# Handing x and the norm weights over with columns on partitions, in a hybrid HGRN2 / latent-attention block on one core

## The reference

```
h   = rms_norm(x, attn_norm_w)
hq, hf, hi, hg, c_q, c_kv, k_r = split(h @ w_in)                 # 4 x 1024, 512, 512, 64
o_a = hgrn2(hq, hf, hi, hg)          # gated linear recurrence, 8 heads of 128, chunks of 64
o_b = latent_attention(rms_norm(c_q, ..) @ w_uq, rms_norm(c_kv, ..) @ w_ukv, k_r)   # 8 heads
x   = x + concat([o_a, o_b]) @ w_out
h   = rms_norm(x, ffn_norm_w)
x   = x + (silu(gate) * up) @ w_down        # gate, up = split(h @ w_gate_up), 5632 each
```

## Time and profile before

| | us |
|---|---|
| median of 3 runs | 1115.05 |
| lowest, highest | 1113.57, 1115.18 |
| the profiled execution | 1115.01 |
| its span from first to last instruction | 1113.3 |
| PE busy | 1103.5 |
| DVE busy | 900.2 |
| ACT busy | 644.7 |
| POOL busy | 61.0 |
| DMA, mean rate over the span | 207 GB/s |

### The profile page before, as it was taken

How to read it: one execution, slowest core, us unless ns; L and a number is a source line. 1 busy time by engine, 2 the same in 40 slices (tenths; PEclk the granted TensorE clock), 3 DMA queues, 4 the chain that set the end, 5 groups by cost and what they waited for, 6 DMA issues and landing times.

```text
span 1113.3 us, 15363 instructions
## 1 busy us (share of the span) xinstructions
PE 1103.5 (99%) x5176; PEld 927.6 (83%) x5176; DVE 900.2 (81%) x1234; ACT 644.7 (58%) x910; POOL 61.0 (5%) x154
## 2 busy tenths in 40 slices
PE   8999999999999999999999999999999999999998
PEld 7988888888888888888888888888888878888887
DVE  6688787587876577588988888988988889999887
ACT  7566777668654466365455555554554555655553
POOL 4200000000000000000000000000000020000000
PEclk9999999999999999999999999999999999999999
DMA  8766455554655455767777777787777786666665
GB/s 269 209 187 200 146 169 157 157 162 152 230 183 172 164 176 171 227 218 224 234 236 225 228 233 220 230 240 218 233 237 228 233 290 210 200 215 202 197 205 170
DMA packets 107557, 230.01 MB, mean 207 GB/s; under 512 B 8265, under 2 KB 19314, under 8 KB 107250
## 3 DMA queue, kind: packets, MB, share of 16 engines
q1 hardware_dynamic: 101346, 209.30, 60.3%
q0 software_dynamic: 5856, 19.93, 5.7%
q10 hardware_dynamic: 304, 0.14, 0.0%
HBM read 218.85 MB, written 10.49 MB: 206 GB/s over the span
## 4 chain that ended last, share of the span: by engine, by line
PE 91%; DVE 4%; DMA 2%; ACT 1%; issue 1%; SPq 0%; DVEq 0%; ACTq 0%
PE side L1975 22%; PE main L1731 20%; PE side L1977 11%; PE main L1734 10%; PE side L1945 4%; PE side L1946 4%; PE side L1947 4%; PE main L1945 3%; PE main L1946 3%; PE main L1947 3%; DMA raw<-in_w_down 1%; PE main L1751 1%; PE side L1773 1%; DVE w_lo L1122 1%; PE side L1870 1%
## 5 line engine op out<-in xcount | busy, mean ns | idle before, releaser
L1013 ACT CAST w_hi<-raw 128x1024 fp32r<-128x1024 f32 x245 | 239.8, 984 | 162.8 <-PE side L1975 62.8
L1573 DVE TENSOR_TENSOR w_lo<-raw,w_hi 128x1024 fp32r<-128x1024 f32 x245 | 274.6, 1133 | 17.7 <-ACT w_hi L1013 17.5
L1122 DVE TENSOR_TENSOR w_lo<-raw,w_hi 128x1024 fp32r<-128x1024 f32 (+3 forms) x156 | 178.8, 1156 | 97.1 <-ACT w_hi L793 94.4
L793 ACT CAST w_hi<-raw 128x1024 fp32r<-128x1024 f32 (+3 forms) x156 | 153.4, 993 | 130.2 <-PE main L1731 125.4
L1731 PE MATMUL main<-w_hi,hT_hi 128*128 128x512 f32 (+2 forms) x416 | 161.2, 388 | 0.2 <-issue 0.2
L1734 PE MATMUL main<-w_hi,hT_lo 128*128 128x512 f32 (+2 forms) x416 | 157.6, 380 | 0.0
L1975 PE MATMUL side<-w_hi,hT_hi 128*128 128x512 f32 x400 | 155.6, 389 | 0.0
L1977 PE MATMUL side<-w_hi,hT_lo 128*128 128x512 f32 x400 | 155.6, 389 | 0.0
L1731 PE MATMUL main<-w_lo,hT_hi 128*128 128x512 f32 (+2 forms) x416 | 107.1, 379 | 0.0
L1975 PE MATMUL side<-w_lo,hT_hi 128*128 128x512 f32 x400 | 106.9, 389 | 0.0
L1731 PEld LDWEIGHTS main<-w_hi,hT_hi 128*128 128x128 f32 x416 | 78.2, 188 | 13.2 <-issue 0.4
(11 more groups left out here) (292 smaller groups left out, 1887.5 us busy)
## 6 DMA issues: line engine op xcount, KB each, us to landing
raw<-in_w_gate_up SPq DMA_DIRECT2D x176, 512.0 KB, 4.8
raw<-in_w_down SPq DMA_DIRECT2D x88, 512.0 KB, 4.5
raw<-in_w_in SPq DMA_DIRECT2D x64, 512.0 KB, 4.0
raw<-in_w_out SPq DMA_DIRECT2D x32, 512.0 KB, 3.6
raw<-in_w_in SPq DMA_DIRECT2D x15, 384.0 KB, 5.0
squares<-hiddenT POOLq DMA_DIRECT2D x11, 512.0 KB, 5.3
hiddenT<-squares POOLq DMA_DIRECT2D x44, 128.0 KB, 5.2
raw<-in_w_ukv SPq DMA_DIRECT2D x8, 512.0 KB, 4.0
```

The source lines that it names most:

```text
L793: copy(w_hi[:, slot, 0:n], raw[:, slot, 0:n]).then_inc(s_hi, 1)
L1013: copy(w_hi[:, n % RING, 0:cols], src).then_inc(s_hi, 1)
L1122: tt(w_lo[:, slot, 0:n], raw[:, slot, 0:n], w_hi[:, slot, 0:n].bitcast(F32), ALU.subtract)\
L1573: tt(w_lo[:, n % RING, 0:cols], src, w_hi[:, n % RING, 0:cols].bitcast(F32), ALU.subtract)\
```

## The change

The host hands over a further array, `columns` (128 x 4137): for each partition 41 norm weights (attn, ffn, q latent, kv latent, hgrn) and then x with its columns on partitions, 16 tiles of 256 tokens. It is loaded in nine pieces into the place of `hT_lo`; the norm weights land in `vec_cols` with the first piece. ACT makes `hT_hi` from it and DVE makes `hT_lo` in place, so step `x` has no part for PE, and both steps `vec` are gone. The weights of g0 are issued by ACT, beside the first piece by SP. The load of g2 stands one place further ahead in SP's order.

`X` in rows is still needed for the squares and for the residual. It is loaded in four chunks of 512 columns behind g11, g12, g14 and g16; `sq1` moves to positions 10, 12, 13 and 15, `r1a` and `r1b` to 16 and 17. Since `lat_in` of block 0 (position 11) is now ahead of `r_in`, it copies; the squares of `lat_a` are scaled by `r_in`, and `lat_b` multiplies by both factors. The small loads that are left (positions, q_head and k_head weights) go behind g18, g19 and g20.

`sums_in` waits for a count of its own before each of the ten token sums (`SUMS_FROM`), where it waited once for each chunk (0, 2, 4, 6, 8 granules into the down projection).

```
+SUMS_FROM = (0, 0, 4, 8, 13, 19, 25, 31, 37, 43)
...
-X_AFTER = {1: (2,), 2: (3,), 3: (4,), 4: (5,), 5: (6,), 6: (7,), 7: (8,)}
-
-X_TURNED = (FIRST, -1, 1, 2, 3, 4, 5, 6, 7)
+XT_AFTER = {1: (1,), 2: (2,), 3: (3, 4), 4: (5,), 5: (6,), 6: (7,), 7: (8,)}
+X_AFTER = {11: 0, 12: 1, 14: 2, 16: 3}
+SMALL_AFTER = 18
...
-    s = [(FIRST, ("vec", 0))] + [(at, ("x", p)) for p, at in enumerate(X_TURNED)]
-    s += [(2 * c + 3, ("sq1", c)) for c in range(4)]
-    s += [(10, ("r1a",)), (11, ("r1b",)), (19, ("vec", 1))]
+    s = [(at, ("sq1", c)) for c, at in enumerate((10, 12, 13, 15))]
+    s += [(16, ("r1a",)), (17, ("r1b",))]
...
+        def load_tokens(p):
 
             k, wide = PIECES[p]
-            cols = slice(P * k, P * (k + wide))
-            engine.dma_start(X[:, :, cols], x_v[:, :, cols]).then_inc(s_x[p], 16)
+            c0, c1 = V_ROWS + SEQ * k if p else 0, V_ROWS + SEQ * (k + wide)
+            nc.sync.dma_start(x_columns[:, c0:c1], columns[:, c0:c1]).then_inc(s_xt[p], 16)
...
-            load_x(sp, 0)
-            for g, (b, k, n) in enumerate(GRANULES):
-                kind, i, w, c0, cols, rows, _ = BLOCKS[b]
+            load_tokens(0)
+            for g in range(1, G0):
...
+                for p in XT_AFTER.get(g, ()):
+                    load_tokens(p)
+
+                if g in X_AFTER:
+                    cols = slice(NB * X_AFTER[g], NB * (X_AFTER[g] + 1))
+                    sp.dma_start(X[:, :, cols], x_v[:, :, cols]).then_inc(s_x[X_AFTER[g]], 16)
...
-            pool.wait_ge(s_x[len(PIECES) - 1], 16)
+            pool.wait_ge(s_x[3], 16)
...
-                pool.wait_ge(s_used, W1 + 2 * c)
                 for n, p in enumerate(CHUNKS[c]):
+                    pool.wait_ge(s_used, W1 + SUMS_FROM[p])
...
-                elif kind == "x":
-                    ps, (k, wide) = filled(s), PIECES[a[0]]
-                    split_hi([(hT_hi[:, k + n, :], ps[:, n * SEQ:(n + 1) * SEQ], V_ATTN + k + n) for n in range(wide)])
+                if kind == "x":
+                    k, wide = PIECES[a[0]]
+                    act.wait_ge(s_xt[a[0]], 16)
+                    split_hi([(hT_hi[:, k + n, :], x_turned(k + n), V_ATTN + k + n) for n in range(wide)])
...
-                        square(latents[i][:, t, :], sumsq[:, t:t + 1])
+                        square(latents[i][:, t, :], sumsq[:, t:t + 1], scale=r_in[:, t:t + 1])
...
-            act.dma_start(vec_rows[0:KT, :], attn_norm_w.rearrange("a (k p) -> (a k) p", p=P)).then_inc(s_attn, 16)
-            load_x(act, 1)
+            load_granule(act, 0)
...
+                    for n in range(k, k + wide):
+                        ins = stt(out=hT_lo[:, n, :], in0=x_turned(n), scalar=vec_cols[:, V_ATTN + n:V_ATTN + n + 1],
+                                  in1=hT_hi[:, n, :].bitcast(F32), op0=ALU.mult, op1=ALU.subtract)
...
-                        ts(v, v, inv[:, t:t + 1], None, ALU.mult).then_inc(s_lat, 1)
+                        ts(v, v, inv[:, t:t + 1], r_in[:, t:t + 1], ALU.mult, ALU.mult).then_inc(s_lat, 1)
```

More of the change, by code:

```diff
@@ L274, in schedule @@
     s += [(e + 3, ("r2a",)), (e + 4, ("r2b",))]
+    s += [(at, ("x", p)) for p, at in enumerate(X_SPLIT)]
     return sorted(s, key=lambda x: x[0])
@@ L290, in steps_at @@
     return [step for p, step in SCHEDULE if p == position]
-def split_steps_at(position):
-    own = [step for step in steps_at(position) if step[0] != "x"]
-    return own + [("x", p) for p, at in enumerate(X_SPLIT) if at == position]
 def side_uses(step):
     kind = step[0]
-    if kind in ("x", "x2", "lat_t", "o_t"):
+    if kind in ("x2", "lat_t", "o_t"):
         return [(step, "dve")]
-    if kind in ("vec", "turn", "probs_t", "join7", "join8"):
+    if kind in ("turn", "probs_t", "join7", "join8"):
         return [(step, "act")]
@@ L359, in split_needed, with hybrid_layer @@
     return SPLIT[("x", len(PIECES) - 1)] + 1
-def hybrid_layer(nc, x, positions, attn_norm_w, w_in, hgrn_lb, hgrn_norm_w, mla_q_norm_w, w_uq, mla_kv_norm_w,
-                 w_ukv, q_head_norm_w, k_head_norm_w, w_out, ffn_norm_w, w_gate_up, w_down, out):
+def hybrid_layer(nc, x, columns, positions, w_in, hgrn_lb, w_uq, w_ukv, q_head_norm_w, k_head_norm_w, w_out, w_gate_up,
+                 w_down, out):
     weights = {"w_in": w_in[0], "w_uq": w_uq[0], "w_ukv": w_ukv[0], "w_out": w_out[0]}
@@ L381, in hybrid_layer @@
         hT_hi = sb("hT_hi", [P, KT, SEQ], F32R)
+        loaded = ctx.enter_context(ExitStack())
+        x_columns = sb("x_columns", [P, GAP + KT * SEQ], F32, loaded)[:, GAP - V_ROWS:]
+        loaded.close()
+        sb("vec_cols", [P, GAP])
+        vec_cols = x_columns[:, 0:V_ROWS]
         hT_lo = sb("hT_lo", [P, KT, SEQ], F32R)
@@ L494, in hybrid_layer @@
         s_tlo = sem("s_tlo")
-        s_x = [sem(f"s_x{p}") for p in range(len(PIECES))]
-        s_attn = sem("s_attn")
+        s_xt = [sem(f"s_xt{p}") for p in range(len(PIECES))]
+        s_x = [sem(f"s_x{c}") for c in range(4)]
         s_small = sem("s_small")
@@ L1050, in _ @@
                     convert(n % RING, loads(n), n, granule_size(n))
-                for s in split_steps_at(g):
+                for s in steps_at(g):
                     step(s)
@@ L1777, in step @@
                 kind, a = s[0], s[1:]
[L1778 to L1792 removed]
+                if kind == "x2":
                     c, j = a
@@ L1914, in lhs_of @@
                 return (mT_hi, mT_lo, ks) if kind == "uq" else (hT_hi, hT_lo, ks)
-            for g in range(FIRST, 0):
-                for s in steps_at(g):
-                    step(s)
             for g, (b, k, n) in enumerate(GRANULES):
@@ L2068, in granule_size @@
     return n * BLOCKS[b][4]
-_INS = ["x", "positions", "attn_norm_w", "w_in", "hgrn_lb", "hgrn_norm_w", "mla_q_norm_w", "w_uq", "mla_kv_norm_w",
-        "w_ukv", "q_head_norm_w", "k_head_norm_w", "w_out", "ffn_norm_w", "w_gate_up", "w_down"]
+_INS = ["x", "columns", "positions", "w_in", "hgrn_lb", "w_uq", "w_ukv", "q_head_norm_w", "k_head_norm_w", "w_out",
+        "w_gate_up", "w_down"]
 def kernel(**inputs):
@@ L2081 @@
     rows = np.concatenate([np.arange(P), np.arange(SEQ - 1, P - 1, -1)])
+    laid = {**inputs, "x": inputs["x"][:, rows], "positions": inputs["positions"][:, rows]}
+    norms = [inputs[f"{n}_w"][0].reshape(-1, P).T
+             for n in ("attn_norm", "ffn_norm", "mla_q_norm", "mla_kv_norm", "hgrn_norm")]
+    x_columns = laid["x"][0].T.reshape(KT, P, SEQ).transpose(1, 0, 2).reshape(P, KT * SEQ)
+    laid["columns"] = np.concatenate(norms + [x_columns], axis=1)
     for name in _INS:
-        a = np.ascontiguousarray(inputs[name][:, rows] if name in ("x", "positions") else inputs[name])
+        a = np.ascontiguousarray(laid[name])
         arrays[f"in_{name}"] = a
```

70 lines of the change are left out of this document (26 added, 44 removed).

## The result

| | us |
|---|---|
| kernel before, median (lowest to highest) | 1114.37 (1113.41 to 1115.18) |
| changed kernel, median (lowest to highest) | 1120.82 (1119.56 to 1121.52) |
| ratio, 95% interval | 1.0055 [1.0043, 1.0067] |
| profiled execution before, and its span | 1115.01, 1113.3 |
| profiled execution after, and its span | 1121.52, 1119.8 |

A forecast was written before the change was run, and what follows sets the result against it. TensorE, busy 1103.5 of 1113.3 us, was taken as the bound. Gains of 3.0 (start), 0.26 (norm-weight transpose) and 1.3 (token sums), 4.56 us in all, from 1115.0 gave 1110.5 us, range 1109.0 to 1112.8.

The forecast's parts named there:

- Term 1: Start, first lat block: without the transposes of x, lat 1 begins at 24.5 for 27.53, a gain of 3.0 us.
- the 7.95 that the bytes gave: Start: 236 KB less ahead of w_in for g2, 0.65 us at 373 GB/s, so it lands at 7.95, not 8.60.
- The rule of the Trainium skill that spoke against it: Loads of x: rows off 256 B boundaries need an extra transaction, an estimated 0.4 us; left out of the sum.
- The first matmul of all: Sign at the start: TensorE's first matmul was to come before 4.6 us.
- rival (a): Start: TensorE stays longer at its lower clock, g2 at 0.32 us a matmul, 1112.0 to 1112.3 us; chance 0.17.
- the seven granules' 2.08 us each: First lat block from g2 on: seven undisturbed granules on TensorE at 2.08 us each, 14.56 us.
- Term 2: After the pass at 47.09: the second transpose of norm weights goes, a gain of 0.26 us in full.
- Part 3: Lat blocks: x rows loaded later, squares later, r_in applied later, GpSimd starting at about 33 us; cost 0.
- rival (c): First lat block: holes keep TensorE at its lower clock, 1.8 us more per granule, 1117.6 with four; chance 0.04.
- Term 3: Head of the down projection: token sums loaded singly no longer delay w_down; gain 1.3 us, between 0.3 and 1.8.
- Rival (d): Lat blocks: x rows come late and ScalarE stands at the squares, two us at most, 1112.5 us; chance 0.06.

The follow-up runs named there:

- the start alone: Changed kernel with hT_lo 256 bytes on, GpSimd released by the last x piece in columns, token sums' loads at their old wait: 1111.22 us, ratio 0.9974.
- the kernel with the load early: Changed kernel with hT_lo 256 bytes on and GpSimd's 512 KB load of hgrn_lb released by the last x piece in columns: 1112.5 us, ratio 0.9985.
- the place mended: Changed kernel with hT_lo 256 bytes further on than before the change, not 192 (gap of 64 floats): 1113.06 us, ratio 0.9989.
- the kernel with both edits: Changed kernel with hT_lo 256 bytes on and GpSimd released by the last x piece in columns: 1110.18 us, ratio 0.9958.
- POOL early alone: Changed kernel with GpSimd waiting for the last piece of x in columns, not the last chunk in rows: 1118.01 us, ratio 1.0032.

## Why the prediction was wrong

**Term 1, the start: right, and a little too small.** Forecast 3.0 us with g9 at 24.5; it came at 24.14, and alone it is worth 3.2 us. w_in for g2 was on chip at 6.99 us (the start of its cast), not at the 7.95 that the bytes gave:

```profile
6.99 0.83 ACT L802 CAST w_hi<-raw 128x768 fp32r<-128x768 f32 x1 [1.15 <-DMA raw<-in_w_in]
8.11 0.91 ACT L849 ACTIVATE hT_hi<-x_columns 128x256 fp32r<-128x256 f32 x2 [0.30 <-DMA x_columns<-in_columns]
```

The piece of x behind it then became the last thing to arrive, so of these 1.6 us only 1.2 reached PE (9.16 for 10.34). The rule of the Trainium skill that spoke against it (page "DMA: Bandwidth & Descriptors", section "How a descriptor splits into AXI transactions") left no mark on this start: by it the term would have been 2.6 us, and from 12 to 15 us, with the new rows of x among the loads, the DMAs moved 384 GB/s for the 373 of the earlier trace rows. The first matmul of all came at 4.93, not before 4.6; it mattered nothing, as the working said. Matmuls in g2 took 0.21 us, then 0.18, and not 0.32: rival (a) did not occur in this execution. It did in others. With the start alone the first pass of g2 went at 0.31 us a matmul, and in the kernel with the load early all of g2 went at 0.32 us or more, so that lat 1 began 2.35 us later than here:

```profile
11.20 1.49 PE L1763 MATMUL main<-w_hi,hT_lo 128*128 128x384 f32 x4
...
26.49 0.33 PE L1743 MATMUL main<-w_hi,hT_hi 128*128 128x384 f32 x1
```

So the start's gain varies from run to run. Of the seven granules' 2.08 us each became 2.11; that was the place of `hT_lo` (with the place mended it is 2.08 again), visible here and not in my sum.

**Term 2, 0.26 us: right.** From the start of that pass to the next product it is 44.65 - 44.07 = 0.58 us now, where it was 47.94 - 47.09 = 0.85. It is inside the 3.2 us of the start alone.

**Part 3 failed, at its last sentence**: "so it is done by 33 + 17 = 50; DVE waits for its constants first at 72.87: 0." The time was right (51.55). What was wrong was to ask only who waits for POOL's results. POOL's work has a price for whoever works beside it. Its clears held DVE for 2 us at the one spot where PE comes to DVE's result with no slack left, and its 512 KB load moved among w_in's. The runs price it at 2.8 us (1120.82 to 1118.01), most of it the clears (2.2). The working also missed that this slack itself had shrunk. Before, `lat` was ready at 50.79 + 0.88 = 51.67 for a PE that came at 53.33. With the start 3 us sooner PE comes near 50.1, but DVE begins to scale `lat` only 1.0 us sooner, at 49.77. Even with nothing held there are 0.59 us of wait left in the kernel with both edits; in the one with POOL early alone there are none.

The Trainium skill has the rule that I should have weighed here, on the page "SBUF — State Buffer", section "SBUF: two separate sides": VectorE and GpSimd share one pair of SBUF ports. VectorE needs it in its two-port modes, which a TENSOR_SCALAR can enter, or with two inputs in SBUF, and then only against a GpSimd instruction that reads SBUF. Whoever starts first has the pair for a whole instruction, and the other is blocked. The traces agree. The held instructions are each a TENSOR_SCALAR within SBUF, and in one case it ended with the second clear (51.97 and 51.94). The `w_lo` subtraction has two inputs in SBUF, but a clear reads nothing, and it kept its 1.23 us. One thing goes beyond the rule as stated: the held instruction sat out both clears, 1.37 and 0.95 us, not one.

**The clock, rival (c), was the right mechanism at the wrong place.** I looked for gaps in lat 0 that would put PE at its lower level and gave it 0.04. It happened behind the wait of 2.36 us at 52 us, for about 3 us of time, and there a matmul of 320 columns starts every 0.27 us for 0.147. That is some 1.4 us of the 3.8 in the profiled execution (12 matmuls by 0.12), and a part of why this loss varies from run to run.

**No term at all for the place of `hT_lo`: the step that decided.** The change part lists what is removed, added and moved among instructions and transfers. That a tile moves by 192 bytes was nowhere costed, although it was in the code. It is 7.8 us, more than all the gains together. The ledger of the 6.45 us between the medians: -3.2 for the start, -1.05 for the sums, +2.8 for POOL, +7.8 for the place, sum +6.35.

**Term 3, the token sums: mechanism partly right, size under the forecast.** In the profiled execution it was worth 1.8 us (82 matmuls to 90), within the range that I gave. Over the runs it is 1.05 us with an interval down to none. The mistake was to take one execution's stall as fixed: another one of a kernel with the same instructions had none.

**The rest.** Rival (d), late rows of x, did not occur as such: ACT's squares stood in no wait. With the two faults mended the change gives 1110.18 us, within 0.4 us of the forecast, and beats both kernels. It lies 0.42% under the kernel before.

## What to carry to other kernels

Compare where the tiles lie before and after a change, not only the instructions: the place of a matmul's operands in their partition counts, of the stationary one and of the streamed one. Keep it as it was modulo 256 bytes when a tile is put ahead of them; a pad of 64 bytes that did so repaired 7.8 us here. When an off-path engine is released later, ask whose instructions its work will then lie beside, and whether one of them is on the path; "nobody waits for it yet" does not make it free. And a stall read in one profiled execution may be missing in the next: before its removal is counted in full, the spread of the runs should allow it.

## What the runs showed of the hardware

- A matmul of 128x512 in float32r whose stationary tile begins 64 bytes past a multiple of 128, with the streamed one on such a multiple, takes 394 ns by the trace instead of 389, the one ahead of it 392. 32 bytes past, they take 398 and 396 (the place alone, on the kernel before). With the streamed operand 64 bytes off and the stationary one not, all take 394. The rise in time of the kernel is 7 to 8, 16 and 24.5 us. ScalarE's cast, VectorE's subtraction and the loads of `raw` keep their times. Whether the step is 128 or 256 bytes, and whether the distance between the two operands is what counts, is open. The loss is small from 60 to 399 us (0.7 us) and even from there to 871 us (6.5 us). In part that is because fewer matmuls have `hT_lo` there (267 for 610), but each of them costs about 2.6 ns there and 10.6 later, and why was not settled.
- A clear on GpSimd (0.95 to 1.4 us) holds a VectorE TENSOR_SCALAR from SBUF to SBUF until it and the clear queued behind it end, to within 0.3 us by the trace: 2.36 us for 0.17. It leaves a subtraction of two SBUF tiles (1.23 us) and a TENSOR_SCALAR out of PSUM (0.62 us) as they were.
- A wait of TensorE of 2.36 us, in a stretch in which it had been busy without a gap, was followed by about 3 us at 1.2 GHz, one of 3.46 us by about 6 us. Waits of 0.59 us (both mended) and of 0.71 us were not followed by a lower granted clock in the windows.
